# First projection of a two-layer hybrid diffusion backbone: order of loads, three blocks split, low weights by VectorE two blocks ahead

## The chip, the cores and the metric

One core of a Trainium2 chip runs the whole network in one launch. The metric is the device time in microseconds (us); smaller is better. The engines named are TensorE (PE), VectorE (DVE), ScalarE (ACT), GpSimd (POOL) and SyncE (SP), whose queue issues the loads.

## The reference

512 latent tokens (x) and 256 context tokens (ctx), width 1024, two layers, all in float32. Each layer is a mixer and a SwiGLU of 2816, each behind an RMS norm whose result is shifted and scaled by a modulation computed from a conditioning vector, one for x and another for the context. Layer 0's mixer is half gated linear attention in both directions, half grouped attention with rotary positions; layer 1's is windowed attention.

```python
mod_x = (sc @ ada_w[l] + ada_b[l])[:, None, :]        # sc = silu(c); mod_c from c_ctx
sh1x, sc1x, g1x, sh2x, sc2x, g2x = jnp.split(mod_x, 6, axis=-1)
hx = modulate(rms_norm(x, norm1_g[l]), sh1x, sc1x)    # h * (1 + scale) + shift
hc = modulate(rms_norm(xc, norm1_g[l]), sh1c, sc1c)
...
gq, gkk, gv, gg, lr_f, lr_b, bq, bk, bv = split_cols(h @ w_in, EVEN_WIDTHS)
dec_f = jax.nn.log_sigmoid((lr_f @ gk_w[0] + gk_b[0]).astype(jnp.float32)) / GLA_TAU
```

## The kernel before

The network is a stream of weight blocks of 128 output columns (`BLOCKS`), numbered n; layer 0's input projection is blocks 0 to 18 (`FIRST[("out", 0)]` is 19). Activations lie transposed, features on partitions, tokens along the free axis; a block multiplies eight 128x128 weight tiles with all 768 tokens and 2 columns that carry the shifts. Float32 accuracy comes from three products of rounded halves: each operand is split into a high part (a cast, `fp32r`) and a low part (operand minus high part). So a block is 8 x 3 products on 770 columns.

For each block: SP loads the raw weights into a ring of three (`load_raw`, L512); ScalarE casts the high part (`high`, L650); GpSimd subtracts the low part (L619), in place over the raw weights; TensorE multiplies (`block_products`, L1724) into one of two PSUM tiles `lin`; VectorE evacuates with the norm's factor (`scaled_out`, L1114 and L1115); ScalarE adds the shift's share (`mixer_projection`, L728). Block n+2 waits for block n's evacuation (`ev`).

The norm's factor is applied after the product, so that products can start before it is known. At the start the modulation is made in four groups (`ada_mm` L1669, two 1 MB loads each; `ada_copy` L657; `ada_T` L1679; `ada_reduce` L1050); the first two give the scale (`mod_scale`, `modA`, L1081). ScalarE casts the scaled x tiles (L702, L706), VectorE makes their low parts (L1126, L1131), and `first_blocks` (L1744) multiplies blocks 0 and 1, latent tokens (part 0) first, context tokens and shift columns (part 1) after the mean square (`mean_square`, L1777). Squares are L664, their sums L1091.

The rest of the modulation ("late tiles") is made on VectorE beside the projections: `late_modulation` (L1066), two products of 128x1024 for a tile in layer 0, with `c_activated` (L719) ahead on ScalarE. `LATE_AT` says how many of them stand in each block: before the evacuation from block 5 on, behind it up to block 4. Their loads (`load_late`, L525) use a ring of three, so tile i waits on SP until tile i-3 is done, and the raw load behind it in SP's order waits too.

Between blocks run the parts of the linear attention: `logits` (PE L1997; ACT L749, L750), `minus_exponential` (L754), `logarithm` (L758), `decays` and `references` on VectorE (L1368 to L1384), `relative` (L600) and `queries_scaled` (L608) on GpSimd, `bounded` (L1389), `exponentials` (L762, L763), transposes of values (L2003) and keys (L2009), `means` (L2015) and roots for the heads' norms (L785, L787), `given` (L1277) for the states handed to each chunk. Each engine runs its instructions strictly in the order in which they are written; the order around each block is written by hand with the block's number.

## Time and profile before

| | |
|---|---|
| median of 3 runs | 1618.42 us (1618.2 to 1618.67) |
| the profiled execution | 1620.3 us, span 1618.5 us |
| TensorE busy | 1557.9 us, 96% of the span |
| VectorE, ScalarE, GpSimd busy | 887.0, 544.6, 591.7 us |
| first block product | 23.49 us |
| first projection's blocks 2 to 18 | 49.7 to about 228 us |

A profile is one execution; the table's spans are of that one. Engines' timelines are read as: start, duration, engine and line, operation, what it writes and reads, how often, and in brackets how long the engine was idle before and what ended that. The kernel's later parts (attention, SwiGLU, layer 1) are not touched by the change, except where the given states are made.

### The profile page before, as it was taken

To read this page: it belongs to the slowest core of one execution; us is meant where nothing else is said; L and a number is where in the kernel's file an instruction comes from. 1 tells how busy PE (TensorE), PEld (TensorE's weight loads), DVE (VectorE), ACT (ScalarE), POOL (GpSimd) and SP (SyncE) were. 2 spreads that over 40 slices of the span, in tenths; PEclk is the share of its full clock that TensorE was granted. 3 is DMA by queue.
4 is the path that set the end of the run, shared out by engine and by line. 5 is a ranking of instruction groups with operands and counts; after the bars stand their busy time and mean duration, and the time that the engine had idled before them with its cause. 6 is when DMAs were issued, how large, how long until landed. Compare 5 with 4: busy or idle time off the path is not lost.

```text
span 1618.5 us, 25145 instructions
## 1 busy us (share of the span) xinstructions
PE 1557.9 (96%) x10716; PEld 1285.7 (79%) x10716; DVE 887.0 (55%) x1250; ACT 544.6 (34%) x711; POOL 591.7 (37%) x263
## 2 busy tenths in 40 slices
PE   6999999889999999999999999999999999999997
PEld 3887764467888888888888888865579998998995
DVE  5699776568577766665566433666643221221324
ACT  4743424453422211221122233245544322322232
POOL 1263235602333222322222222355644444444442
PEclk9999999999999999999999999999999999999998
DMA  8523110034233333333433222200022222223232
GB/s 340 197 104 118 41 40 1 1 133 143 71 116 127 131 130 115 119 131 130 144 120 127 92 75 69 66 27 1 1 66 86 95 95 91 92 92 104 92 97 99
DMA packets 41775, 158.54 MB, mean 98 GB/s; under 512 B 4768, under 2 KB 5152, under 8 KB 39872
## 3 DMA queue, kind: packets, MB, share of 16 engines
q1 hardware_dynamic: 41232, 156.74, 28.1%
q8 instruction: 85, 1.39, 0.4%
q0 software_dynamic: 432, 0.20, 0.1%
q14 instruction: 26, 0.21, 0.0%
HBM read 154.95 MB, written 2.10 MB: 97 GB/s over the span
## 4 chain that ended last, share of the span: by engine, by line
PE 72%; DVE 3%; issue 2%; ACT 1%; POOL 1%; DVEq 0%; POOLq 0%
PE psum L1724 65%; PE psum L1928 2%; PE psum L1896 1%; DVE osb L1305 1%; PE psum L1829 1%; POOL acc L593 1%; DVE product L1066 0%; PE psum L1944 0%; DVE mx L1200 0%; PE psum L1913 0%; PE psum L1902 0%; PE psum L1900 0%; PE psum L1898 0%; DVE xT L1547 0%; PE psum L1801 0%
## 5 line engine op out<-in xcount | busy, mean ns | idle before, releaser
L1724 PE MATMUL psum<-act,whi 128*128 128x258 f32 (+2 forms) x4000 | 792.1, 318 | 6.6 <-DVE xT L1547 4.5
L619 POOL TENSOR_TENSOR wlo<-raw,whi 128x1024 fp32r<-128x1024 f32 (+1 forms) x181 | 443.6, 2451 | 917.7 <-ACT whi L650 917.7
L1724 PEld LDWEIGHTS psum<-act,whi 128*128 128x128 f32 x4000 | 592.9, 189 | 66.7 <-issue 11.7
L1724 PE MATMUL psum<-act,wlo 128*128 128x512 f32 (+1 forms) x2000 | 476.3, 317 | 0.0
L1066 DVE SCALAR_TENSOR_TENSOR product<-adr,cb 128x1024 f32<-128x1024 f32 x128 | 281.8, 2234 | 134.9 <-DMA adr<-adat_dram 129.5
L1724 PEld LDWEIGHTS psum<-act,wlo 128*128 128x128 f32 x2000 | 311.5, 189 | 27.1
L650 ACT ACTIVATE whi<-raw 128x1024 fp32r<-128x1024 f32 (+1 forms) x181 | 188.1, 1039 | 330.2 <-DMA raw<-weights_dram 329.8
L1114 DVE SCALAR_TENSOR_TENSOR tmps<-psum,rs 128x256 f32<-128x256 f32 (+1 forms) x176 | 78.1, 485 | 199.7 <-PE psum L1724 195.2
L1724 PE MATMUL psum<-gh,whi 128*128 128x512 f32 (+1 forms) x528 | 160.9, 358 | 0.0
L1724 PE MATMUL psum<-gh,wlo 128*128 128x512 f32 (+1 forms) x528 | 160.8, 359 | 0.0
L1724 PE MATMUL psum<-gl,whi 128*128 128x512 f32 (+1 forms) x528 | 159.3, 355 | 0.0
L1547 DVE SCALAR_TENSOR_TENSOR xT<-psum,mod,xT 128x512 f32<-128x512 f32 x96 | 60.4, 656 | 160.2 <-PE psum L1724 155.7
L1200 DVE TENSOR_REDUCE mx<-psum 128x4 f32<-128x1024 f32 (+2 forms) x68 | 78.8, 1159 | 49.3 <-PE psum L1829 37.7
L1006 ACT ACTIVATE gh<-tmps 128x768 fp32r<-128x768 f32 (+1 forms) x44 | 32.5, 739 | 211.2 <-DVE tmps L1627 211.2
L593 POOL TENSOR_TENSOR acc<-acc,probT 128x1024 f32<-128x1024 f32 (+2 forms) x47 | 90.8, 1931 | 27.1 <-ACT probT L886 22.2
L1724 PEld LDWEIGHTS psum<-gh,whi 128*128 128x128 f32 x528 | 87.8, 188 | 15.9
L1724 PEld LDWEIGHTS psum<-gl,whi 128*128 128x128 f32 x528 | 87.1, 188 | 16.5
L1724 PEld LDWEIGHTS psum<-gh,wlo 128*128 128x128 f32 x528 | 86.7, 188 | 15.4
L1002 ACT ACTIVATE tmps<-tmps,bsm 128x512 f32<-128x512 f32 x66 | 40.7, 648 | 151.1 <-DVE bsm L1115 151.1
L886 ACT ACTIVATE probT<-psum 128x1024 f32<-128x1024 f32 (+2 forms) x80 | 66.9, 848 | 62.1 <-PE psum L1902 42.8
L1928 PE MATMUL psum<-probT,vtok 128*64 128x512 f32 (+2 forms) x320 | 72.6, 532 | 1.9 <-ACT probT L886 1.2
L728 ACT ACTIVATE big<-big,bsm 128x512 f32<-128x512 f32 (+1 forms) x50 | 29.3, 626 | 98.1 <-DVE bsm L1115 98.1
(185 smaller groups left out, 1212.2 us busy)
## 6 DMA issues: line engine op xcount, KB each, us to landing
raw<-weights_dram SPq DMA_DIRECT2D x181, 512.0 KB, 3.5
adr<-adat_dram SPq DMA_DIRECT2D x80, 512.0 KB, 4.5
ada_w<-ada_dram SPq DMA_DIRECT2D x8, 1024.0 KB, 15.1
xT<-x_in_dram SPq DMA_DIRECT2D x4, 1536.0 KB, 13.2
cb<-crow_dram SPq DMA_DIRECT2D x2, 1024.0 KB, 8.5
out_dram<-big SPq DMA_DIRECT2D x8, 256.0 KB, 2.1
con<-consts_dram SPq DMA_DIRECT2D x1, 512.0 KB, 7.4
con<-consts_dram SPq DMA_DIRECT2D x1, 320.0 KB, 3.5
```

The costliest lines, as they stand in the source:

```text
L593: nc.gpsimd.tensor_tensor(acc[L][:, :, qa:qb], so_far, probT[L][:, t % NPT, :, qa:qb], ALU.add) \
L619: nc.gpsimd.tensor_tensor(wlo[:, s, 0:w], raw[:, s, 0:w], whi[:, s, 0:w].bitcast(F32), ALU.subtract).then_inc(sem("s_lo"), 1)
L650: A(whi[:, s, 0:w], raw[:, s, 0:w], ACT.Copy).then_inc(sem("s_hi"), 1)
L886: A(probT[L][:, t % NPT, :, qa:qb], scored[t % 2][:, :, qa:qb], ACT.Exp, scale=SCALE) \
L1002: last = A(t, t, ACT.Silu, bias=bsm[:, n % 4, c:c + 1])
L1006: A(gh[L][:, b["i"], 0:b["tok"]], tmps[:, 6 + b["h"] % 2, 0:b["tok"]], ACT.Copy) \
L1066: STT(out=products[t % 2][:, :], in0=w, scalar=1.0, in1=cb[:, c, :], op0=ALU.mult, op1=ALU.mult, accum_out=mod[:, layer, d, c:c + 1]).then ...
L1114: STT(out=tiles[:, a:e], in0=ps, scalar=factor, in1=rs[:, a:e], op0=ALU.mult, op1=ALU.mult)
L1200: V.reduce_max(mx[:, i % 3, piece["slot"], rows_, :].rearrange("p q g -> p g q"), s_, AX.X) .then_inc(sem("a_mx"), 1)
L1547: ins = STT(out=xT[:, m, a:e], in0=lin[n % 2][:, a:e], scalar=mod[:, L, gate + m, c:c + 1], in1=xT[:, m, a:e], op0=ALU.mult, op1=ALU.add)
L1724: last = MM(out_[:, o:o + t1 - t0], w_, a_[:, t0:t1], start=k == order[0] and j == 0, stop=k == order[-1] and j == 2)
L1928: last = MM(bank(6)[r, qa:qb], vtok[L][:, kt, r], probT[L][:, t % NPT, g, qa:qb], start=a == 0, stop=a == len(u["steps"]) - 1, skip_group_ ...
```

## The change

- Loads: x and the context are loaded apart, x's 512 columns first and in two halves of the tiles, the first half in front of the second pair of modulation loads; raw weights 0 to 2 come earlier.
- Raw weights 3 go to a place of their own (`stage`), so they don't wait for the ring.
- The modulation groups use one half of one PSUM tile each (`wk[0]`), so group c waits for group c-1's copy and reduction; `wk[1]` holds block 2's first products.
- Scale and x tiles are made by halves: after the first group, tiles 0 to 3; after the second, 4 to 7. Blocks 0, 1 and 2 are all multiplied in parts by `first_blocks`, between the modulation groups.
- Low weights of blocks 0 to 18 are made on VectorE (`weights_low`), those of block n+2 behind the evacuation of block n and in front of block n's late tiles where n is below 5; GpSimd makes them from block 19 on.
- Logits, exponentials and logarithms of the decays come one block later; decays and references move behind the evacuation of blocks 5 and 6; the copies into `lrs` and `gks` likewise in block 2.
- `LATE_AT` spreads the 16 late tiles otherwise. `given` is made by halves, the last two halves still at the start of the attention.

```diff
@@ -42,7 +42,7 @@
 LATE = [(0, d) for d in [*range(16, 24), *range(32, 40), *range(24, 32), *range(40, 48)]] + [(1, d) for d in range(48)]
-LATE_AT = [0, 0, 3, 3, 1, 0, 0, 1, 1, 0, 2, 2, 2, 1, 0, 0, 0, 0, 0]
+LATE_AT = [0, 0, 2, 3, 2, 0, 0, 2, 2, 1, 1, 1, 1, 1, 0, 0, 0, 0, 0]
@@ -301,6 +301,7 @@
         gates = big[:, 8:12, :]
+        stage = at("stage", [P, KT * P], G + 14 * TILE)
@@ -421,9 +422,11 @@
+        first_out = [lin[0], lin[1], wk[1]]
...
-            ps = lin[n % 2]
+            ps = first_out[n] if n < 3 else lin[n % 2]
@@ -529,23 +532,28 @@
             x_tiles = x_in.rearrange("p (k t) -> p k t", k=KT)
-            for h in range(ADA_RING):
-                load_ada(h)
+            load_ada(0)
+            load_ada(1)
             load_raw(0)
-            sp.dma_start(xT[:, 0:half, :], x_tiles[:, 0:half, :]).then_inc(sem("s_xa"), 16)
-            sp.dma_start(xT[:, half:KT, :], x_tiles[:, half:KT, :]).then_inc(sem("s_xb"), 16)
+            sp.dma_start(xT[:, 0:half, 0:NX], x_tiles[:, 0:half, 0:NX]).then_inc(sem("s_xa"), 16)
             load_raw(1)
+            load_raw(2)
+            load_ada(2)
+            load_ada(3)
+            sp.dma_start(xT[:, half:KT, 0:NX], x_tiles[:, half:KT, 0:NX]).then_inc(sem("s_xb"), 16)
+            sp.dma_start(xT[:, :, NX:T], x_tiles[:, :, NX:T]).then_inc(sem("s_xc"), 16)
...
                 load_ada(h)
-            load_raw(2)
+            sp.dma_start(stage[:, :], weights[RING, :, :]).then_inc(sem("s_stage"), 16)
             sp.wait_ge(sem("s_adamm"), 2 * len(ADA_EARLY))
+            sp.dma_start(gkw[0:32, :], gkw_in).then_inc(sem("s_rope"), 16)
...
             sp.dma_start(con[:, 0:CC_ID], consts[:, 0:CC_ID]).then_inc(sem("s_rope"), 16)
-            sp.dma_start(gkw[0:32, :], gkw_in).then_inc(sem("s_rope"), 16)
             for n in range(RING, NB):
-                load_raw(n)
+                if n > RING:
+                    load_raw(n)
@@ -615,9 +623,10 @@
                 w = BLOCKS[n]["nk"] * P
-                pool.wait_ge(sem("s_hi"), n + 1)
-                nc.gpsimd.tensor_tensor(wlo[:, s, 0:w], raw[:, s, 0:w], whi[:, s, 0:w].bitcast(F32),
-                                        ALU.subtract).then_inc(sem("s_lo"), 1)
+                if n >= FIRST[("out", 0)]:
+                    pool.wait_ge(sem("s_hi"), n + 1)
+                    nc.gpsimd.tensor_tensor(wlo[:, s, 0:w], raw[:, s, 0:w], whi[:, s, 0:w].bitcast(F32),
+                                            ALU.subtract).then_inc(sem("s_lo"), 1)
@@ -644,17 +653,20 @@
                 w = BLOCKS[n]["nk"] * P
-                act.wait_ge(sem(f"s_raw{s}"), 16 * (n // RING + 1))
+                if n == RING:
+                    act.wait_ge(sem("s_stage"), 16)
+                else:
+                    act.wait_ge(sem(f"s_raw{s}"), 16 * (n // RING + (0 if s == 0 and n > RING else 1)))
...
                     act.wait_ge(sem("s_acc"), n - RING + 1)
-                A(whi[:, s, 0:w], raw[:, s, 0:w], ACT.Copy).then_inc(sem("s_hi"), 1)
+                A(whi[:, s, 0:w], stage[:, :] if n == RING else raw[:, s, 0:w], ACT.Copy).then_inc(sem("s_hi"), 1)
...
                     act.wait_ge(sem("s_adaT"), c - 1)
-                A(adasb[:, c % 2, :], wk[0][:, 512 * (c % 2):512 * (c % 2) + 512], ACT.Copy) \
+                A(adasb[:, c % 2, :], wk[0][:, 0:512], ACT.Copy) \
@@ -693,20 +705,23 @@
             ada_copy(0)
-            ada_copy(1)
             high(0)
-            act.wait_ge(sem("s_modA"), 1)
...
                 if k % 4 == 0:
+                    act.wait_ge(sem("s_modA"), 2 if k else 1)
...
                     .then_inc(sem("s_nhx"), 1)
-            high(1)
+                if k == 3:
+                    high(1)
+                    high(2)
+                    ada_copy(1)
+            act.wait_ge(sem("s_xc"), 16)
...
             for k in range(KT):
-                if k == 2:
+                if k == 4:
@@ -793,15 +808,14 @@
                     nc.scalar.preload_act_table_set(LN_EXP)
-                if n in (2, 3):
-                    logits(2 * n - 4)
-                    logits(2 * n - 3)
-                if n in (2, 3):
-                    minus_exponential(2 * n - 4)
-                    minus_exponential(2 * n - 3)
                 if n in (3, 4):
-                    logarithm(2 * n - 6)
-                    logarithm(2 * n - 5)
+                    logits(2 * n - 6)
+                    logits(2 * n - 5)
+                    minus_exponential(2 * n - 6)
+                    minus_exponential(2 * n - 5)
+                if n in (4, 5):
+                    logarithm(2 * n - 8)
+                    logarithm(2 * n - 7)
@@ -975,7 +989,10 @@
                     attention(1)
-                high(n + 2)
+                if n == 0:
+                    high(RING)
+                if n >= 3:
+                    high(n + 2)
@@ -991,6 +1008,8 @@
                         mixer_projection(L, n, b)
+                    if n == 1:
+                        high(n + 3)
@@ -1115,16 +1134,28 @@
             dve.wait_ge(sem("s_par"), 16)
-            for c in range(2):
-                ada_reduce(c)
-            dve.wait_ge(sem("s_mod"), 2)
-            mod_scale(0)
-            dve.wait_ge(sem("s_modA"), 1)
-            for k in range(KT):
-                hi, lo = [act_tile("proj", 0, k, low) for low in range(2)]
-                dve.wait_ge(sem("s_nhx"), k + 1)
-                STT(out=lo[:, 0:NX], in0=xT[:, k, 0:NX], scalar=modA[:, 0, k, 0:1], in1=hi[:, 0:NX].bitcast(F32),
-                    op0=ALU.mult, op1=ALU.subtract).then_inc(sem("s_nlx"), 1)
+            def weights_low(n):
+                s = n % RING
+                dve.wait_ge(sem("s_hi"), n + 1)
+                TT(wlo[:, s, :], stage[:, :] if n == RING else raw[:, s, :], whi[:, s, :].bitcast(F32), ALU.subtract) \
+                    .then_inc(sem("s_lo"), 1)
+            for h in range(2):
+                ada_reduce(h)
+                dve.wait_ge(sem("s_mod"), h + 1)
+                mod_scale(0, 4 * h, 4 * h + 4)
+                if h == 0:
+                    weights_low(0)
+                dve.wait_ge(sem("s_modA"), h + 1)
+                for k in range(4 * h, 4 * h + 4):
+                    hi, lo = [act_tile("proj", 0, k, low) for low in range(2)]
+                    dve.wait_ge(sem("s_nhx"), k + 1)
+                    STT(out=lo[:, 0:NX], in0=xT[:, k, 0:NX], scalar=modA[:, 0, k, 0:1], in1=hi[:, 0:NX].bitcast(F32),
+                        op0=ALU.mult, op1=ALU.subtract).then_inc(sem("s_nlx"), 1)
+                if h == 0:
+                    weights_low(1)
+                    weights_low(2)
@@ -1133,9 +1164,10 @@
                     dve.wait_ge(*nq("sq", 0, 1))
+                if k == 4:
+                    ada_reduce(2)
                 add_square(0, k, T)
-            for c in range(2, 4):
-                ada_reduce(c)
+            ada_reduce(3)
@@ -1268,14 +1300,13 @@
-            def given(d):
-                dve.wait_ge(sem("g_carry"), 2 * d + 2)
-                if d == 1:
-                    dve.wait_ge(sem("g_sr"), 1)
-                ref_ = gpos[:, 0, 2 * d:2 * d + 2, 1:NCH].unsqueeze(3).to_broadcast([P, 2, NCH - 1, CH])
-                TT(statr[d][:, 1:NCH, :, :].rearrange("p c g v -> p g c v"),
-                   states[d][:, :, :, 0:NCH - 1].rearrange("p g v c -> p g c v"), ref_, ALU.mult) \
+            def given(d, g):
+                dve.wait_ge(sem("g_carry"), 2 * d + g + 1)
+                if d == 1 and g == 0:
+                    dve.wait_ge(sem("g_sr"), 2)
+                ref_ = gpos[:, 0, 2 * d + g, 1:NCH].unsqueeze(2).to_broadcast([P, NCH - 1, CH])
+                TT(statr[d][:, 1:NCH, g, :], states[d][:, g, :, 0:NCH - 1].rearrange("p v c -> p c v"), ref_, ALU.mult) \
@@ -1402,13 +1434,6 @@
-                if n == 2:
-                    low_rank_low()
-                if n in (5, 6):
-                    for i in (2 * n - 10, 2 * n - 9):
-                        decays(i)
-                    for i in (2 * n - 10, 2 * n - 9):
-                        references(i)
@@ -1564,6 +1591,8 @@
                     dve.wait_ge(*nq("rs", q, 1))
+                if n == 1:
+                    weights_low(RING)
@@ -1594,9 +1623,18 @@
                     scaled_out(n, proj_tile(L, m), DK ** -0.5 if L == 0 and m in (3, 4) else 1.0)
+                    if n == 2:
+                        low_rank_low()
+                    if 2 <= n < FIRST[("out", 0)] - 2:
+                        weights_low(n + 2)
...
                             late_modulation(i)
+                    if n in (5, 6):
+                        for i in (2 * n - 10, 2 * n - 9):
+                            decays(i)
+                        for i in (2 * n - 10, 2 * n - 9):
+                            references(i)
@@ -1660,23 +1698,23 @@
-                if c >= 2:
-                    pe.wait_ge(sem("s_adacp"), c - 1)
+                if c >= 1:
+                    pe.wait_ge(sem("s_adacp"), c)
...
                     for g in range(4):
-                        last = MM(wk[0][32 * g:32 * g + 32, 512 * (c % 2):512 * (c % 2) + 512],
+                        last = MM(wk[0][32 * g:32 * g + 32, 0:512],
...
                 pe.wait_ge(sem("s_adacp"), c + 1)
-                if c >= 2:
-                    pe.wait_ge(sem("s_mod"), c - 1)
+                if c >= 1:
+                    pe.wait_ge(sem("s_mod"), c)
                 for q in range(4):
-                    last = TR(wk[1][:, 512 * (c % 2) + P * q:512 * (c % 2) + P * q + P],
+                    last = TR(wk[0][:, 512 + P * q:512 + P * q + P],
@@ -1725,16 +1763,16 @@
-            def first_blocks(n, part):
-                out_ = lin[n % 2]
+            def first_blocks(n, part, tiles=range(KT)):
+                out_ = first_out[n]
...
                     pe.wait_ge(sem("s_shift"), 2)
-                for k in range(KT):
+                for k in tiles:
@@ -1780,18 +1820,25 @@
             ada_mm(0)
+            ada_T(0)
+            first_blocks(0, 0, range(0, 4))
             ada_mm(1)
-            ada_T(0)
+            first_blocks(1, 0, range(0, 2))
             ada_T(1)
-            first_blocks(0, 0)
+            first_blocks(1, 0, range(2, 4))
+            first_blocks(2, 0, range(0, 4))
+            first_blocks(0, 0, range(4, 8))
             ada_mm(2)
-            first_blocks(1, 0)
+            first_blocks(1, 0, range(4, 6))
+            ada_T(2)
+            first_blocks(1, 0, range(6, 8))
             ada_mm(3)
-            ada_T(2)
+            first_blocks(2, 0, range(4, 6))
             ada_T(3)
+            first_blocks(2, 0, range(6, 8))
             mean_square(0, T)
-            first_blocks(0, 1)
-            first_blocks(1, 1)
+            for n in range(3):
+                first_blocks(n, 1)
@@ -2018,9 +2065,11 @@
-                if n in (2, 3):
-                    logits(2 * n - 4)
-                    logits(2 * n - 3)
+                if n in (3, 4):
+                    logits(2 * n - 6)
+                    if n == 3:
+                        pe.wait_ge(*ev(2))
+                    logits(2 * n - 5)
```

## Rows read from the trace of the kernel before

**Rows 1.** The page: busy time by engine, and the chain that ended last by line.
```profile
PE 1557.9 (96%) x10716; PEld 1285.7 (79%) x10716; DVE 887.0 (55%) x1250; ACT 544.6 (34%) x711; POOL 591.7 (37%) x263
...
PE psum L1724 65%; PE psum L1928 2%; PE psum L1896 1%; DVE osb L1305 1%; PE psum L1829 1%; POOL acc L593 1%; DVE product L1066 0%; PE psum L1944 0%; DVE mx L1200 0%; PE psum L1913 0%; PE psum L1902 0%; PE psum L1900 0%; PE psum L1898 0%; DVE xT L1547 0%; PE psum L1801 0%
```

**Rows 2.** A stretch of the start: busy time by engine, granted clock, DMA share, GB/s.
```profile
23.40:28.00 4.60, 4.51 (x11) 3.57 (x12) 4.59 (x7) 4.53 (x8) 0.01 (x1) 0.50 1.02 422
```

**Rows 3.** TensorE's timeline, from the modulation to block 3.
```profile
10.72 1.93 PE L1669 MATMUL psum<-ada_w,cpad 128*32 128x512 f32 x8 [0.71 <-DMA ada_w<-ada_dram]
...
23.49 1.19 PE L1744 MATMUL psum<-act,whi 128*128 128x512 f32 x2 [4.45 <-DVE act L1126]
...
31.43 1.92 PE L1669 MATMUL psum<-ada_w,cpad 128*32 128x512 f32 x16
...
42.18 1.46 PE L1777 MATMUL psum<-big,con 128*128 128x512 f32 x4
43.45 0.51 PE L1744 MATMUL psum<-act,whi 128*128 128x258 f32 x2
...
49.74 0.95 PE L1724 MATMUL psum<-act,whi 128*128 128x512 f32 x4 [0.25 <-issue]
...
59.02 0.86 PE L1724 MATMUL psum<-act,whi 128*128 128x512 f32 x4
```

**Rows 4.** TensorE's timeline: its six waits from block 5 to block 13.
```profile
77.71 0.94 PE L1724 MATMUL psum<-act,whi 128*128 128x512 f32 x4 [0.88 <-issue]
...
87.02 0.95 PE L1724 MATMUL psum<-act,whi 128*128 128x512 f32 x4 [0.60 <-ACT whi L650]
...
104.62 0.94 PE L1724 MATMUL psum<-act,whi 128*128 128x512 f32 x4 [0.41 <-DVE bsm L1115]
...
142.46 0.87 PE L2009 MATMUL psum<-con,gsc 128*128 128x128 f32 x6 [1.89 <-ACT hrs L787]
...
152.27 0.87 PE L2009 MATMUL psum<-con,gsc 128*128 128x128 f32 x6 [1.07 <-DVE vtok L1181]
...
165.97 0.88 PE L2009 MATMUL psum<-con,gsc 128*128 128x128 f32 x6 [2.40 <-ACT kgt L773]
```

**Rows 5.** VectorE's timeline: late tiles, decays, evacuation of block 7.
```profile
59.51 1.21 DVE L1066 SCALAR_TENSOR_TENSOR product<-adr,cb 128x1024 f32<-128x1024 f32 x1
...
61.79 3.42 DVE L1066 SCALAR_TENSOR_TENSOR product<-adr,cb 128x1024 f32<-128x1024 f32 x1
...
93.01 0.94 DVE L1368 SCALAR_TENSOR_TENSOR dec<-dec,gsc 128x768 f32<-128x768 f32 x1
94.05 1.76 DVE L1376 TENSOR_TENSOR_SCAN gsc<-cmask,dec 128x768 f32<-128x768 f32 x1
...
107.62 1.02 DVE L1114 SCALAR_TENSOR_TENSOR big<-psum,rs 128x512 f32<-128x512 f32 x2
```

**Rows 6.** ScalarE's timeline: x tiles, c's activation, logits, the cast of weights 5.
```profile
21.76 5.20 ACT L702 ACTIVATE act<-xT,modA 128x512 fp32r<-128x512 f32 x8 [2.48 <-DVE modA L1081]
...
56.77 1.92 ACT L719 ACTIVATE cb<-cb 128x2048 f32<-128x2048 f32 x1
...
61.98 0.89 ACT L749 ACTIVATE gsc<-psum,par 128x768 f32<-128x768 f32 x1
...
73.90 1.07 ACT L650 ACTIVATE whi<-raw 128x1024 fp32r<-128x1024 f32 x1 [7.20 <-DMA raw<-weights_dram]
```

**Rows 7.** GpSimd's timeline: the subtraction of weights 5, two decay differences.
```profile
75.04 2.57 POOL L619 TENSOR_TENSOR wlo<-raw,whi 128x1024 fp32r<-128x1024 f32 x1 [10.92 <-ACT whi L650]
...
97.96 5.07 POOL L600 TENSOR_TENSOR dec<-gsc,gd 128x768 f32<-128x768 f32 x2
```

**Rows 8.** SP's timeline (late tiles, raw weights 5), and the page's raw loads.
```profile
61.91 7.11 SPq L525 DMA_DIRECT2D adr<-adat_dram  x3
69.06 0.43 SPq L512 DMA_DIRECT2D raw<-weights_dram  x1
...
raw<-weights_dram SPq DMA_DIRECT2D x181, 512.0 KB, 3.5
```

27 lines of the change are left out of this document (16 added, 11 removed).

## The prediction

> **What bounds the kernel now.** I read the page's busy line and its chain that ended last first [rows 1]: TensorE is busy 96% of the span, and its block products (L1724) alone are 65% of the chain. So a change in the first projection is worth what it takes from, or adds to, TensorE's idle time and its start, and nothing else. Then I read the timelines of the first 170 us, engine by engine.
>
> The start: TensorE has modulation matmuls while the first weights of the modulation stream in (10.72), then waits 4.45 us for VectorE's first low tile and begins the first block at 23.49; from there it is busy almost without a break to block 2 at 49.74 and block 3 at 59.02 [rows 3]. Its clock is at the lower level, 0.50, in 23.4 to 28 us [rows 2]. After block 3 it waits six times, 7.3 us in all: 0.88, 0.60, 0.41, 1.89, 1.07 and 2.40 us [rows 4]. The last three wait for ScalarE or VectorE copies that come late because VectorE evacuated the blocks late. That VectorE is late is to be seen in its timeline: from 59.5 us on it runs almost without a pause; block 8 waits 0.41 us for the evacuation of block 6, whose products were over 9 us before, and block 7 is evacuated at 107.62 [rows 4, 5]. So VectorE is nearly co-critical from block 3 to block 13; that is where this change decides.
>
> **The start, worked out.** The DMA engines move 422 GB/s in this stretch [rows 2], about 2.5 us for 1 MB. In the new order the first half of x's latent columns lands at about 14.5 us, raw weights 1 and 2 by 17, the third and fourth modulation loads by 22. The first modulation group (ends 12.7 [rows 3]), its copy, transposes and reduction take about 2.3 us, so modA's first half is there at 15.0. ScalarE then casts x tiles at 0.65 us each (5.20 for 8) [rows 6]. VectorE puts the first low weights in front (1.15 us, below), so its first low x tile ends at 16.9 and TensorE starts block 0 at 17.1, 6.4 us before the 23.49 of now. What moves behind that start: the second modulation group (16 matmul records, 1.92 us at the full clock) and its transposes (0.7 us). What is new is block 2's latent part there. TensorE from 17.1: twelve matmuls at the lower clock at 0.43 us (5.1; 11 in 4.6 us [rows 2]), then sixty at 0.23 (14.0; block 2's 24 products of 770 columns take 8.5 us, 512 of them 0.23 each), three modulation groups (5.8), three sets of transposes (2.2), the mean square (1.3, 42.18 to 43.45), three context parts of 2.9 us each (49.34 less 43.45 is two of them; 8.8) [rows 3], and about 0.6 us of waiting for the third copy, which stands behind four squares on ScalarE. End: 17.1 + 37.8 = 54.9. Block 3 began at 59.02 with 0.72 us of logits in front of it, which now come later; without them 58.3. The front gains 3.4 us. Its bounds: if the copies behind the squares are later, 2 us less; if the clock rises sooner, 1.5 us more.
>
> **The vector queue, worked out.** Removed: nineteen subtractions on GpSimd (2.4 us each), which were off the path but held VectorE: a 1024-wide two-input operation takes 1.21 us alone and 3.42 us beside one of them [rows 5]. Added: the same subtraction on VectorE, an operation this engine does not show at this width. Bounds: 1.15 us apart by the two-input rows of the same width, 2.4 us as on GpSimd; I take 1.15, the same engine and width. Per block VectorE pays 1.15 and is spared up to 2.2. GpSimd's four decay differences (5.07 for two) and four query products stay [rows 7], and by the same comparison I charge about 1.2 us for each where VectorE has two-input work; with none of it, 9.4 us less.
>
> But each subtraction waits on VectorE for ScalarE's cast, and behind it stand the late modulation tiles (2.3 us each, two products of 1.15). Those tiles release the next loads on SP's queue, which lie in front of the next raw load: a ring through SP, DMA, ScalarE and VectorE. Now SP shows it: three tile loads stretched over 7.11 us, the raw load only at 69.06, landed at 73.90, 4.8 us later (median of the kernel 3.5) [rows 8]; ScalarE waits 7.20 us for it [rows 6], but VectorE does not. Followed through:
> - Block 2 ends at 54.7. c's activation on ScalarE stands behind the load of block 4's weights (issued at 51.8) and ends at 59.6 (58.7 now) [rows 6]. Tiles 0 and 1: to 64.2. Block 3 (ends 63.4) evacuated at 65.2.
> - Raw weights 5 are issued at 64.7, land at 69.5, are cast at 70.6. VectorE stands 5.4 us. Subtraction to 71.8, tiles 2 to 4 to 78.7, block 4 evacuated at 79.7.
> - Raw weights 6 are issued once tile 3 is done (76.4) and land at 81.6; cast 82.7. VectorE stands 3.0 us. Subtraction 83.9 (block 6 can start: 87.02 now), tiles 5, 6 to 88.5, block 5 at 89.5.
> - The cast of weights 7 stands behind an evacuation, four logits operations (0.78 apart), two exponentials and two logarithms: 91.2. VectorE stands 1.7 us; subtraction 92.4.
> - Decays of two (2 x 2.7) and references (0.5): 98.3 [rows 5]. Block 6 evacuated 99.3, subtraction with GpSimd beside it 101.7, decays 108.7, clamps 110.9, tiles 7, 8 with GpSimd 116.6, block 7 evacuated 117.6. Now that ends at 108.6 [rows 5].
>
> TensorE needs block 7 evacuated for block 9, and its own low weights 1.2 us later. Its idle time: 1.9 us in front of block 5 (the third and fourth logits need ScalarE's copies of the first two, which stand behind the cast at 70.6), 0.3 at block 6, 1.0 at block 8 (102.0), then, its block 8 ending at 110.6, 8.2 us at block 9 (118.8; 113.1 now). Behind it 1.8, 1.0 and 0.3 us for the value transposes and the mean, whose inputs come from blocks 8 and 9 evacuated late. By block 11 only one late tile stands in each block instead of two, VectorE has caught up, and the 1.89, 1.07 and 2.40 us of now are gone: the first key transposes of block 13 come at about 169.5 against 165.97. In all -3.4 (front) + 14.5 (new idle) - 7.3 (idle of now) = +3.8 us.
>
> A stall of 8 us has a second price. Behind the 4.45 us wait that ended at 23.49 the granted clock is 0.50, the lower of its two levels (1.2 and 2.4 GHz), for some 5 us of matmuls [rows 2, 3]. Behind 8.2 us I expect the lower level again: about 2.4 us lost in block 9, of which 1.8 lie under the wait for the value transposes: +0.5. The trace agrees with a rule of the Trainium skill, page "TensorE: Matmul & The Clock Gate", section "Part 1: The HAM clock gate": the throttled clock is the default, and activity releases it. The rule speaks against this change.
>
> **Edits costed at nothing.** The given states by halves: the same elements, two instructions for one (0.1 us more each), in blocks 17 and 18 where VectorE pauses and TensorE does not wait. The ring's "place" for weights 3 moves no work. gkw before c's rows: 64 KB. The late tiles' new order keeps their number, 16.
>
> **Total.** The profiled run took 1620.3 us with a span of 1618.5; the median is 1618.42, the span's own size, so I add the difference to the median: 1618.4 + 3.8 + 0.5 = 1622.7, said as 1622.5.
>
> **The rivals.**
> - The vector queue keeps up (B). If raw weights land in the median 3.5 us, GpSimd's eight operations cost VectorE nothing and the new waits shrink, block 7 is evacuated at about 111 and block 9 starts near 112 to 114. Following the same chain, the first key transposes of block 13 come about 4.6 us before 165.97: 1613.8. For it: GpSimd's subtractions cost VectorE up to 2.2 us each now, and all go. Against it: the 4.8 us landing and the stretched 7.11 us were seen behind the same loads. With no new wait at all it would be 1618.4 - 3.4 - 7.3 = 1607.7; nothing shows how SP could be that early.
> - The two cancel (C): block 9 starts at about 115 to 116, the front's 3.4 us are given back and no more: 1618.
> - Slower for good (D): the stall not only at block 9 but the backlog lasting beyond block 13. It decides if a subtraction takes nearer to 2.4 than to 1.15 us: 1.25 more in some eight blocks is 10 us of vector work, of which about half comes through: 1627.5.
> - The change does not do what it says: TensorE's first block does not start earlier, since the loads of x land later than worked out, with block 0 at 20 instead of 17.1. Then 2.9 us more of A, inside the range.
>
> **How the numbers follow.** A (forecast, 1622.5, own range 1619 to 1626) 0.50; B 0.22; C 0.20; D 0.08. A measurement of this kernel can tell about 0.2% from no change, 3.2 us: faster is below 1615.2, slower above 1621.7. Of A, 0.13 lies below that line. Faster 0.22, same 0.20 + 0.13 = 0.33, slower 0.37 + 0.08 = 0.45. The range reaches down to B's value and a little beyond, up to nearly D's: 1613.5 to 1627. What is left out is the deep end of B and the high side of D.
>
> **What would show it.** In the changed profile: TensorE's first block product at 17.1 (right within 1 us) and block 3 at 54.9; VectorE idle in front of its subtractions, released by ScalarE's cast, 5 us near 65 and 3 us near 80; raw weights 5 cast at about 70; a TensorE wait for VectorE near 110 of about 8 us, with a lower granted clock behind it; the waits of 1.89, 1.07 and 2.40 us gone. If the wait near 110 is under 3 us the forecast is wrong, and then I expect VectorE's own operations at their uncontended lengths, and block 9 before 114. If block 3 comes later than 56.5, the front was over-priced.

## The result and the profile of the changed kernel

| | before | changed |
|---|---|---|
| time, median (range), us | 1618.51 (1618.2 to 1619.24) | 1624.71 (1622.38 to 1626.09) |
| ratio, 95% interval | | 1.0035 [1.0023, 1.0046] |
| profiled execution: time, span, us | 1620.3, 1618.5 | 1622.38, 1620.3 |

The changed kernel is slower by 0.35%, about 5.7 us (the medians differ by 6.2). The forecast was 1622.5 (own range 1619 to 1626). The profiled execution is the lowest of the changed kernel's five, so the two traces show less of a difference (1.8 us of span) than the medians.

The page: busy time, the costliest group of TensorE (idle time in front of it, and what ended it), and the median landing of a raw load (last column, us).

```profile
PE 1558.8 (96%) x10716; PEld 1288.2 (80%) x10716; DVE 890.9 (55%) x1272; ACT 544.6 (34%) x711; POOL 539.9 (33%) x244
...
L1762 PE MATMUL psum<-act,whi 128*128 128x258 f32 (+2 forms) x3968 | 788.2, 319 | 11.7 <-DVE wlo L1141 7.3
...
raw<-weights_dram SPq DMA_DIRECT2D x180, 512.0 KB, 3.5
```

Against [rows 1]: TensorE is busy as before, GpSimd 51.8 us and nineteen instructions less, VectorE only 3.9 us more, although it has taken these nineteen subtractions over. The idle time in front of the block products now stands for the most part in one place, 7.3 us.

TensorE's timeline at the start answers to [rows 3]; the two stretches behind it (granted clock third from the end, GB/s last) answer to [rows 2].

```profile
13.27 1.12 PE L1717 MATMUL psum<-con,adasb 128*128 128x128 f32 x4 [0.71 <-ACT adasb L669]
17.02 1.19 PE L1782 MATMUL psum<-act,whi 128*128 128x512 f32 x2 [2.64 <-DVE act L1154]
...
44.63 0.59 PE L1782 MATMUL psum<-act,whi 128*128 128x258 f32 x2
...
53.48 0.75 PE L1762 MATMUL psum<-act,whi 128*128 128x512 f32 x3
```

```profile
17.00:19.70 2.70, 2.68 (x6) 2.15 (x7) 2.70 (x4) 2.57 (x4) 0.00 (x0) 1.00 1.02 425
19.70:23.00 3.30, 3.30 (x23) 1.41 (x21) 1.43 (x2) 0.00 (x0) 0.00 (x0) 1.00 1.00 392
```

The granted clock reads 1.00 in both stretches, and yet the six matmuls of the first lie 0.43 us apart, as under 0.50 in [rows 2]; soon behind 19.7 us they lie 0.23 apart. Here the durations are to be read, not the column.

Block 0 starts at 17.02 instead of 23.49 and block 3 at 53.48 instead of 58.3 (59.02 less 0.72 us of logits, which now stand later). The front gains 4.8 us in this pair of traces. In the seven traces with this start (the changed kernel, e1, e2, e3, e4, e7, e10) block 3 begins at 52.76 to 53.48; in the four with the start of the kernel before (itself, e5, e6, e9) the work in front of it, logits left out, ends at 57.59 to 58.76.

All TensorE waits over 0.3 us from block 3 to block 13; they answer to [rows 4]:

```profile
72.29 0.62 PE L2044 MATMUL psum<-lrs,gks 96*128 96x512 f32 x2 [0.98 <-ACT dec L765]
...
73.87 0.62 PE L2044 MATMUL psum<-lrs,gks 96*128 96x512 f32 x2 [0.97 <-ACT dec L765]
...
117.18 1.62 PE L1762 MATMUL psum<-act,whi 128*128 128x512 f32 x4 [7.26 <-DVE wlo L1141]
...
139.95 0.74 PE L2050 MATMUL psum<-con,big 128*128 128x128 f32 x5 [1.43 <-DVE vgt L1429]
```

Four waits, 10.6 us, where there were six with 7.3 us. The one that matters is block 9's, which waits for its low weights on VectorE. What VectorE did before that answers to [rows 5]:

```profile
69.68 1.23 DVE L1141 TENSOR_TENSOR wlo<-raw,whi 128x1024 fp32r<-128x1024 f32 x1 [5.02 <-ACT whi L662]
...
81.86 1.23 DVE L1141 TENSOR_TENSOR wlo<-raw,whi 128x1024 fp32r<-128x1024 f32 x1 [3.08 <-ACT whi L662]
...
90.09 1.23 DVE L1141 TENSOR_TENSOR wlo<-raw,whi 128x1024 fp32r<-128x1024 f32 x1 [1.42 <-ACT whi L662]
...
98.15 1.55 DVE L1141 TENSOR_TENSOR wlo<-raw,whi 128x1024 fp32r<-128x1024 f32 x1
99.62 2.22 DVE L1400 SCALAR_TENSOR_TENSOR dec<-dec,gsc 128x768 f32<-128x768 f32 x1
...
108.89 2.48 DVE L1085 SCALAR_TENSOR_TENSOR product<-adr,cb 128x1024 f32<-128x1024 f32 x1
...
114.87 1.01 DVE L1133 SCALAR_TENSOR_TENSOR big<-psum,rs 128x512 f32<-128x512 f32 x2
...
115.87 1.21 DVE L1141 TENSOR_TENSOR wlo<-raw,whi 128x1024 fp32r<-128x1024 f32 x1
```

VectorE stands three times, 9.5 us, in front of a subtraction and for ScalarE's cast. From 90.09 on it works without a gap: decays, references, clamps, the late tiles 7 and 8 (107.75 to 114.87), the evacuation of block 7, then block 9's low weights, ready at 117.0. So block 9's start is 90.1 plus 27 us of queue. The casts themselves wait for raw weights, and these for SP (they answer to [rows 6] and [rows 8]):

```profile
68.59 1.06 ACT L662 ACTIVATE whi<-raw 128x1024 fp32r<-128x1024 f32 x1 [7.27 <-DMA raw<-weights_dram]
...
80.77 1.06 ACT L662 ACTIVATE whi<-raw 128x1024 fp32r<-128x1024 f32 x1 [5.49 <-DMA raw<-weights_dram]
```

```profile
51.16 12.85 SPq L528 DMA_DIRECT2D adr<-adat_dram  x3
64.06 0.43 SPq L515 DMA_DIRECT2D raw<-weights_dram  x1
```

SP issues three tile loads, each when VectorE has freed a buffer, over 12.85 us, and only then the raw weights 5, at 64.06; their cast starts at 68.59.

The granted clock of the changed kernel (third figure from the end), behind the two short waits and behind the long one:

```profile
74.00:76.00 2.00, 2.00 (x9) 1.72 (x10) 2.00 (x5) 1.28 (x2) 0.00 (x0) 0.67 0.72 252
76.00:78.00 2.00, 2.00 (x8) 1.71 (x8) 2.00 (x5) 0.00 (x0) 0.00 (x0) 0.50 0.73 209
...
110.00:114.00 4.00, 0.00 (x0) 0.00 (x0) 4.00 (x5) 0.00 (x0) 2.71 (x2) 0.78 0.37 113
114.00:118.00 4.00, 0.82 (x3) 0.76 (x4) 4.00 (x9) 2.02 (x4) 0.09 (x1) 0.50 0.85 301
118.00:124.00 6.00, 6.00 (x24) 5.16 (x24) 6.00 (x6) 2.98 (x4) 5.63 (x2) 0.63 0.34 125
```

What a stretch loses is the time that TensorE was busy times (1 less the clock): 0.7 and 1.0 us from 74 to 78, 0.4 us from 117.2 to 118, 2.2 us from 118 to 124, in all 4.3 us. The kernel before has a clock of 1.00 in every stretch from 28.4 to 239 us.

A mark behind all of this is the same pair of attention matmuls in both kernels, first in the kernel before, then in the changed one:

```profile
239.10 0.44 PE L1852 MATMUL psum<-identr,mxr 128*128 128x128 f32 x2 [1.45 <-DVE mxr L1212]
```

```profile
242.41 0.44 PE L1899 MATMUL psum<-identr,mxr 128*128 128x128 f32 x2 [1.45 <-DVE mxr L1244]
```

From block 3 to that mark, the kernel before (its two logits in front of block 3 left out), then the changed one:

```profile
59.02:239.10 180.08, 170.43 (x1317) 139.92 (x1315) 154.94 (x209) 73.45 (x102) 72.25 (x30) 1.00 0.26 88
```

```profile
53.48:242.41 188.93, 174.97 (x1321) 143.91 (x1319) 155.66 (x228) 78.01 (x106) 30.68 (x15) 0.96 0.25 87
```

The changed kernel is 3.3 us later there. The sum: -4.8 (front) + 10.6 (waits now) - 7.3 (waits before) + 0.9 (small waits, 1.8 against 0.9) + 4.3 (clock) = +3.7 us, 0.4 us more than measured. "The mark" means this place below.

### The profile page after: what moved, and what is told of

Its sections match the earlier page's. It is cut to its first block, busy times and chain, and to the rows that moved or that the text cites. A ratio compares the mean times of both kernels' runs of the same rounds, so it can differ in the third digit from the quotient of the medians.

```text
span 1620.3 us, 25160 instructions
## 1 busy us (share of the span) xinstructions
PE 1558.8 (96%) x10716; PEld 1288.2 (80%) x10716; DVE 890.9 (55%) x1272; ACT 544.6 (34%) x711; POOL 539.9 (33%) x244
## 4 chain that ended last, share of the span: by engine, by line
PE 71%; DVE 3%; issue 2%; ACT 1%; POOL 0%; DVEq 0%; POOLq 0%
PE psum L1762 65%; PE psum L1975 2%; PE psum L1943 1%; DVE osb L1336 1%; PE psum L1876 1%; POOL acc L601 0%; DVE product L1085 0%; PE psum L1991 0%; DVE mx L1232 0%; PE psum L1960 0%; PE psum L1949 0%; PE psum L1947 0%; PE psum L1945 0%; DVE xT L1574 0%; PE psum L1848 0%
## 5 line engine op out<-in xcount | busy, mean ns | idle before, releaser
L628 POOL TENSOR_TENSOR wlo<-raw,whi 128x1024 fp32r<-128x1024 f32 (+1 forms) x162 | 389.6, 2405 | 797.0 <-ACT whi L662 797.0
L1085 DVE SCALAR_TENSOR_TENSOR product<-adr,cb 128x1024 f32<-128x1024 f32 x128 | 278.5, 2208 | 132.2 <-DMA adr<-adat_dram 125.5
```

Of the source, the lines that this page charges most:

```text
L628: nc.gpsimd.tensor_tensor(wlo[:, s, 0:w], raw[:, s, 0:w], whi[:, s, 0:w].bitcast(F32), ALU.subtract).then_inc(sem("s_lo"), 1)
L1085: STT(out=products[t % 2][:, :], in0=w, scalar=1.0, in1=cb[:, c, :], op0=ALU.mult, op1=ALU.mult, accum_out=mod[:, layer, d, c:c + 1]).then ...
```

## The experiments

The theory: the front's gain is given back at block 9, because VectorE's queue up to the evacuation of block 7 is too long. Two things are supposed to make it so: VectorE stands for casts (the ring through SP, DMA, ScalarE and VectorE), and two late tiles stand in block 7 beside GpSimd's differences. The rivals: W, the subtractions are simply too much work for VectorE; that the tiles' places don't matter; H, the order of the loads brings nothing. Each ratio is to the kernel before on the same chip, with the 95% interval.

### e1_raw_first: raw weights ahead of the tiles on SP's queue

```diff
                 if n <= len(LATE_AT):
-                    for i in late_tiles(n - 1):
+                    for i in late_tiles(n - 2):
```

> The changed kernel with one edit on SP's queue: the late tiles of block n-2 instead of n-1 are issued behind the raw load of block n, so a raw load no longer stands behind tile loads that wait for VectorE's products. Theory A (a ring through SP, DMA, ScalarE and VectorE makes VectorE stand 9.5 us): its waits for the casts of weights 5 and 6 (5.0 and 3.1 us) go, the evacuation of block 7 comes about 8 us earlier (107 instead of 114.9), the wait of TensorE at block 9 falls from 7.3 to 2 to 4 us, time 1613 to 1618. Rival W (it is the added vector work, 1.15 us a block, not the waiting): the waits go, but the work behind them fills up, block 9 waits over 6 us, time 1622 or more. Rival F (the split front is itself no gain): no change to speak of in the start, and the time stays above 1618.5 even with the wait at block 9 gone.

1616.91 us (1615.22 to 1619.35), ratio 0.998 [0.9971, 0.9988]; the mark at 233.93. VectorE's subtraction for block 7's weights and TensorE's block 9:

```profile
81.57 1.22 DVE L1141 TENSOR_TENSOR wlo<-raw,whi 128x1024 fp32r<-128x1024 f32 x1
```

```profile
108.66 0.94 PE L1762 MATMUL psum<-act,whi 128*128 128x512 f32 x4 [2.90 <-DVE wlo L1141]
```

From 50 to 120 us none of VectorE's subtractions waits for a cast any more; this one runs at 81.57 and not at 90.09. Block 9's wait falls from 7.26 to 2.90 us. So the ring is a cause, and VectorE does nineteen subtractions in a kernel that is faster than before: W does not hold.

### e4_late_later: no late tile in blocks 7 and 8

```diff
-LATE_AT = [0, 0, 2, 3, 2, 0, 0, 2, 2, 1, 1, 1, 1, 1, 0, 0, 0, 0, 0]
+LATE_AT = [0, 0, 2, 3, 2, 0, 0, 0, 0, 1, 2, 2, 2, 2, 0, 0, 0, 0, 0]
```

> The changed kernel with four late tiles moved out of blocks 7 and 8 into blocks 10 to 13 (0, 0, 2, 3, 2, 0, 0, 0, 0, 1, 2, 2, 2, 2). Theory A: the waits for casts stay (5.0, 3.1, 1.4 us), the evacuation of block 7 comes 4.6 to 7 us earlier (two tiles and what GpSimd adds to them), block 9 waits 0 to 3 us instead of 7.3, TensorE's clock stays at its upper level there, and waits like the 1.89, 1.07 and 2.40 us of before come back at blocks 11 to 13; time 1616 to 1621. Rival W: the same sum of vector work only shifts the wait to blocks 11 to 13, time 1623 or more.

1616.78 us (1614.79 to 1620.08), ratio 0.9981 [0.9972, 0.9989]; the mark at 233.58. The edit takes the two tiles out of block 7 and the two out of block 8, and puts one more into each of blocks 10 to 13. VectorE's cast waits stay as they were (4.88, 2.89 and 1.42 us). TensorE's second logits wait and block 9, and the clock between:

```profile
73.45 0.62 PE L2044 MATMUL psum<-lrs,gks 96*128 96x512 f32 x2 [0.97 <-ACT dec L765]
...
109.74 0.94 PE L1762 MATMUL psum<-act,whi 128*128 128x512 f32 x4 [1.52 <-DVE wlo L1141]
```

```profile
74.00:76.00 2.00, 2.00 (x13) 1.74 (x12) 2.00 (x3) 0.87 (x2) 0.00 (x0) 1.00 0.67 244
```

With the two tiles out of block 7, block 9's wait is 1.52 us although the cast waits remain. So the second cause is shown too, and either cure alone turns the result into a gain of 0.2%. Of the difference between these two traces, 1.7 us are not the edit's: up to block 7 both kernels have the same instructions, and the clock behind the logits waits fell in the one and stayed at 1.00 in the other.

### e10_after_old_tiles: the tile distribution of the kernel before

```diff
-LATE_AT = [0, 0, 2, 3, 2, 0, 0, 2, 2, 1, 1, 1, 1, 1, 0, 0, 0, 0, 0]
+LATE_AT = [0, 0, 3, 3, 1, 0, 0, 1, 1, 0, 2, 2, 2, 1, 0, 0, 0, 0, 0]
```

The entries are blocks 0, 1, 2 and so on. Against the changed kernel one tile more stands in block 2 (three), one less in blocks 4, 7, 8 and 9, and one more in blocks 10 to 12. The text below leaves out blocks 2 and 9 to 12, and its "third tile", which it puts into block 3, is block 2's.

> The changed kernel with the distribution of late tiles of the kernel before (three in block 3, one in block 4, one each in blocks 7 and 8 instead of two). If the stall in front of block 9 is made by the tiles that stand in VectorE's queue ahead of the evacuation of block 7 (theory), one tile and 2.3 to 3.6 us beside GpSimd go from blocks 5 to 8: the wait in front of block 9 shrinks from 7.3 to 3 to 5 us and the total is 1619 to 1622; the wait in front of block 4's or 5's low weights may grow by 1 us, for the third tile stands in block 3 again. If the tiles' places don't matter and the added subtractions do (rival), the wait stays over 7 us and the total at 1624.

1619.07 us (1618.43 to 1621.82), ratio 1.0 [0.9991, 1.0009]; the mark at 237.64.

```profile
90.17 1.22 DVE L1141 TENSOR_TENSOR wlo<-raw,whi 128x1024 fp32r<-128x1024 f32 x1 [1.11 <-ACT whi L662]
...
111.40 1.01 DVE L1133 SCALAR_TENSOR_TENSOR big<-psum,rs 128x512 f32<-128x512 f32 x2
```

```profile
74.83 1.01 PE L2044 MATMUL psum<-lrs,gks 96*128 96x512 f32 x2 [3.82 <-ACT dec L765]
...
113.99 0.94 PE L1762 MATMUL psum<-act,whi 128*128 128x512 f32 x4 [0.70 <-issue]
```

This is the cleanest pair. VectorE's queue starts at the same time (90.17 against 90.09) and has one tile less: block 7 is evacuated 3.47 us earlier (111.40 against 114.87) and block 9 starts 3.2 us earlier. The expected total of 1619 to 1622 was met at its lower edge, block 9's wait (3 to 5 us) was not: it is 0.70, because TensorE itself arrives later. The rival, that the tiles' places don't matter, wanted over 7 us there and does not hold. The third tile in block 2 holds the raw weights on SP longer, ScalarE casts them at 71.14 instead of 68.59, and the logits copies behind this cast cost TensorE 3.82 us. The granted clock behind that wait is 0.70 in 74 to 76 us, 0.50 in 76 to 78 and 0.55 in 78 to 82, worth another 2.9 us. So the change without its new tile distribution is no slower than before; what the front brought is then lost in front of block 5.

### e5_before_spread and e9_before_late_later: the two distributions in the kernel before

```diff
-LATE_AT = [0, 0, 3, 3, 1, 0, 0, 1, 1, 0, 2, 2, 2, 1, 0, 0, 0, 0, 0]
+LATE_AT = [0, 0, 2, 3, 2, 0, 0, 2, 2, 1, 1, 1, 1, 1, 0, 0, 0, 0, 0]   # e5
+LATE_AT = [0, 0, 2, 3, 2, 0, 0, 0, 0, 1, 2, 2, 2, 2, 0, 0, 0, 0, 0]   # e9
```

> The kernel before with the changed kernel's distribution of the late tiles alone (0, 0, 2, 3, 2, 0, 0, 2, 2, 1, 1, 1, 1, 1), all else as before. Theory A (the two tiles in blocks 7 and 8 stand in front of evacuations that TensorE needs): the evacuation of block 7 comes at 110 to 112 instead of 108.6, that of block 8 at 122 to 124 where block 10 wants it at 123.4, the waits of 1.07 and 2.40 us at blocks 12 and 13 shrink since one tile stands there instead of two, in all -1 to +3 us, 1617.5 to 1621.5 on the scale of 1618.5. Rival B2 (the distribution is the gain, and only the subtraction on VectorE spoils it): -3 us or more.

> The kernel before with the later distribution of the late modulation tiles (none in blocks 6 to 8, two each in blocks 10 to 13), nothing else changed. If two tiles in blocks 7 and 8 hurt the changed kernel only because its two decays and its subtractions meet there (theory), the kernel before gains little: its block 7 is evacuated up to 4 us earlier, which takes its wait of 0.41 us in front of block 8 and part of the 1.89, 1.07 and 2.40 us behind, 0 to -4 us, and the two tiles of blocks 12 and 13 give some of it back. If the later distribution is simply better wherever it stands (rival), the gain is the same here as in the changed kernel, -8 us: 1610 to 1612.

e5: 1625.3 us (1624.82 to 1625.68), ratio 1.003 [1.0018, 1.0041]. e9: 1622.23 us (1620.38 to 1623.42), ratio 1.0012 [1.0003, 1.0021]. TensorE in e5, then in e9:

```profile
105.57 1.62 PE L1724 MATMUL psum<-act,whi 128*128 128x512 f32 x4 [2.66 <-DVE bsm L1115]
...
140.60 1.75 PE L2003 MATMUL psum<-con,big 128*128 128x128 f32 x7 [6.10 <-ACT vgt L769]
```

```profile
106.73 0.95 PE L1724 MATMUL psum<-act,whi 128*128 128x512 f32 x4 [2.67 <-DVE bsm L1115]
```

Both expectations missed, on the same side. The distribution of the change costs the kernel before 0.3%, as much as the whole change, where -1 to +3 us was expected, and the rival B2, by which it is a gain, does not hold. The two tiles of block 7 push the evacuation behind them from 107.62 to 114.32, and the copies for the value transposes come 6.10 us late; this wait is not in e9, which has no tile there. The waits of 2.66 and 2.67 us in front of block 8 (0.41 in [rows 4]), and one of 1.12 us in front of block 7, are in both kernels, so they go with what the two distributions share, the tiles of blocks 2 to 4. e9, which helps the changed kernel by 8 us, costs the kernel before about 2 us (ratio 1.0012). So neither distribution is good or bad in itself. Moving tiles moves SP's loads with them; what counts in these traces is which evacuation or cast stands behind them.

### e2_low_last: the subtraction behind the late tiles

```diff
-                    if 2 <= n < FIRST[("out", 0)] - 2:
-                        weights_low(n + 2)
                     if n < 5:
                         for i in late_tiles(n):
                             late_modulation(i)
+                    if 2 <= n < FIRST[("out", 0)] - 2:
+                        weights_low(n + 2)
```

> The changed kernel with one edit on VectorE's queue: in blocks 2 to 4 the subtraction of the low weights stands behind the late tiles, not in front of them; SP's order is as in the changed kernel. Theory A: VectorE does tiles instead of standing; what it wanted of raw weights 5 comes as late as before or a little earlier, VectorE's waits for casts fall from 9.5 to under 2 us in all, the evacuation of block 7 comes 7 to 8 us earlier, block 9 waits 2 to 4 us, time 1614 to 1618. Rival W: as the changed kernel, 1622 or more, since the work is the same. Rival S (the fault is SP's order alone, whatever VectorE does): no gain here, since the raw load still stands behind the tile loads.

1621.14 us (1619.51 to 1624.33), ratio 1.0006 [0.9998, 1.0015]; the mark at 237.58.

```profile
64.59 1.43 PE L1762 MATMUL psum<-act,whi 128*128 128x512 f32 x4 [2.15 <-issue]
...
112.32 1.38 PE L1762 MATMUL psum<-act,whi 128*128 128x512 f32 x4 [2.88 <-DVE wlo L1141]
```

The time is a miss (1614 to 1618 was expected). VectorE's waits for casts are gone and block 9's wait shrank to 2.88 us, both as expected, and with SP's order unchanged the kernel is 0.3% faster than the changed one; so rival S does not hold. But the evacuation of block 7 came 4.9 us sooner and not 7 to 8 (110.01), and block 4's low weights now stand behind two tiles (they run at 63.27, and TensorE waits 2.15 us for them); that was not seen. In this order part of the one wait is traded for the other; e1 has the same wait at block 9 (2.90 us) without the one at block 4, whose weights VectorE subtracts at 56.34 there.

### e3_pool_low: the subtractions back on GpSimd

```diff
-                if n >= FIRST[("out", 0)]:
+                if n >= 4:
                     pool.wait_ge(sem("s_hi"), n + 1)
+                    pool.wait_ge(sem("s_lo"), n)
...
-                    if 2 <= n < FIRST[("out", 0)] - 2:
-                        weights_low(n + 2)
```

> The changed kernel with GpSimd subtracting the low weights from block 4 on, as in the kernel before; the front, SP's order and all else as changed. Theory A: VectorE has nothing that waits for a cast, and pays up to 2.2 us beside each subtraction as before; the 7.3 us wait at block 9 shrinks to 0 to 3, the front's 3.3 us are kept, 1614 to 1617. Rival W: the same or better, since all the added work goes; it can't be told from A by the time alone, but by VectorE's busy time up to block 9: W wants it lower than in the changed kernel, A expects it about the same or higher, as contention replaces the subtractions. Rival F: 1618.5 or more.

1625.24 us (1623.38 to 1629.88), ratio 1.0037 [1.0025, 1.0049]; the mark at 243.20. GpSimd's subtraction, VectorE's product beside it, and block 9:

```profile
69.71 2.91 POOL L629 TENSOR_TENSOR wlo<-raw,whi 128x1024 fp32r<-128x1024 f32 x1 [11.56 <-ACT whi L663]
```

```profile
70.31 3.39 DVE L1086 SCALAR_TENSOR_TENSOR product<-adr,cb 128x1024 f32<-128x1024 f32 x1
```

```profile
114.50 1.62 PE L1761 MATMUL psum<-act,whi 128*128 128x512 f32 x4 [4.58 <-DVE bsm L1135]
```

A miss, and the second run against W. From block 4 on VectorE has no subtraction and no cast wait, and yet the kernel is as slow as the changed one: block 9 still waits 4.58 us, and the value transposes another 3.80. A subtraction on GpSimd stretches the VectorE product beside it from 1.22 to 3.39 us, by 2.2 us, against the 1.15 us that VectorE pays for doing it itself. What VectorE no longer stands, it works: from 58 to 110 us it is busy 48.2 us, in the changed kernel 41.1. So handing the subtractions to VectorE is no loss. The expected 1614 to 1617 was missed because the evacuation of block 7 comes only 1.6 us sooner (113.27 against 114.87), although 9.5 us of waits are gone.

### e6_before_raw_first: e1's edit in the kernel before

```diff
                 if n <= len(LATE_AT):
-                    for i in late_tiles(n - 1):
+                    for i in late_tiles(n - 2):
```

> The kernel before with the edit of e1 on SP's queue (late tiles one block later in SP's order, so raw loads don't stand behind them). Theory A: in the kernel before nothing on VectorE waits for a cast, so only TensorE's waits of 0.88 and 0.60 us at blocks 5 and 6 can go, and ScalarE's 7.2 us wait for raw weights 5; -1.5 to 0 us. Rival G (raw-first is a gain by itself, whatever the order on VectorE, which would make e1's gain of about 9 us against the changed kernel no proof of the ring): -4 us or more.

1619.99 us (1619.03 to 1622.07), ratio 0.9999 [0.999, 1.0008]. TensorE's waits of 0.88 and 0.60 us [rows 4] are gone, and one grew by 0.7 us (0.41 before):

```profile
103.79 0.94 PE L1724 MATMUL psum<-act,whi 128*128 128x512 f32 x4 [1.15 <-DVE bsm L1115]
```

The raw weights were late in the kernel before too, but nothing on VectorE waited for them, so bringing them forward is worth nothing to speak of; rival G, a gain of 4 us or more, does not hold. The wait became one that costs only when the change put a waiting subtraction into VectorE's queue.

### e8_x_later: x behind all four first modulation loads

```diff
-            load_ada(0)
-            load_ada(1)
+            for h in range(ADA_RING):
+                load_ada(h)
             load_raw(0)
...
-            load_ada(2)
-            load_ada(3)
```

> The changed kernel with x's first half loaded behind all four first modulation loads, as before, instead of between them; x and context stay apart and the blocks split. Theory A (the front's gain of 4.8 us up to block 3 rests on x being there at 14.5 us): x's first half lands at about 19.3, block 0 starts at about 21 instead of 17.0, block 3 at 57 to 57.5 instead of 53.5, and since all behind hangs on it the time is 3 to 4.5 us over the changed kernel's, ratio to before 1.0055 to 1.0065. Rival H (the load order is hidden: TensorE makes it up while it waits at block 9 anyway): block 3 comes later but block 9 does not, ratio 1.0035.

1630.74 us (1627.77 to 1631.76), ratio 1.006 [1.0047, 1.0072].

```profile
21.54 1.19 PE L1780 MATMUL psum<-act,whi 128*128 128x512 f32 x2 [7.11 <-DVE act L1152]
...
121.91 1.41 PE L1760 MATMUL psum<-act,whi 128*128 128x512 f32 x3 [8.33 <-DVE wlo L1139]
```

Block 0 starts 4.5 us later, block 9 4.7 us later and the mark 4.7 us later (247.14). The front's gain is real and comes through to the end one for one; H does not hold.

### e7_both: e1 and e4 together

> The changed kernel with both edits of e1 (raw loads ahead of the late tiles) and e4 (no late tiles in blocks 7 and 8, two in 10 to 13). Theory A: both cut the same stall at block 9, so they don't add up in full: no wait at block 9, casts waited for under 1 us in all, about 1 us of waits at blocks 11 to 13; first product of the attention about 9 us before the kernel before, ratio 0.993 to 0.996 (1607.5 to 1612 on the scale of 1618.5). Rival W: the vector work is what it is, the ratio stays at 0.998 like each alone.

1609.91 us (1608.15 to 1611.89), ratio 0.9938 [0.9924, 0.9952]; the mark at 225.91. The group of block products on the page:

```profile
L1762 PE MATMUL psum<-act,whi 128*128 128x258 f32 (+2 forms) x3968 | 784.8, 318 | 4.5 <-DVE xT L1574 4.5
```

From the first block at 16.89 to 219 us TensorE has no wait over 0.3 us. The 4.5 us left in front of the block products stand for something else, far behind. The mark is 13.2 us before that of the kernel before: 4.8 us of front, 7.3 us of old waits, and small parts. This version beats both kernels, by 0.6% and by about 1%. The expectation took the two edits to cut the same stall and not to add up in full; in fact they nearly do (0.55% and 0.54% alone, 0.97% together). Rival W wanted 0.998 here and does not hold; nor does rival F, the front being no gain.

## Why the prediction was right, and where its steps were off

The time, the sign and the mechanism (A) came as forecast: the start earlier, the gain given back in one wait for VectorE in front of block 9. That the sum fits as well as it does (+4.3 against +3.7 us) is in part luck: the new waits were charged at 14.5 us and took 10.6, the clock was charged at 0.5 us and took 4.3, and these two errors cancel. Step by step:

- **Block 0 at 17.1, block 3 at 54.9.** Measured 17.02 and 53.48. The start was right to 0.1 us. The front gained 4.8 us and not 3.4. Block 3 came 36.5 us behind block 0, where 37.8 were charged. The lower clock lasted 2.7 us and not 5.1, the bound "the clock rises sooner", but the 72 products took 19.2 us all the same (19.1 charged): the first twelve 4.35, the other sixty 14.8 and not 14.0. Over-priced were the three sets of transposes (1.1 us, 2.2 charged), the wait for the third copy (0.6 charged, none over 0.2) and the mean square (1.1, 1.3 charged); the modulation groups took 6.2 and not 5.8. In e1, which starts alike, the slow matmuls lasted 4.0 us and block 3 began at 53.32, no later.
- **VectorE's waits of 5.4, 3.0 and 1.7 us.** Measured 5.02, 3.08 and 1.42. Raw weights 5 issued at 64.7 and cast done at 70.6: measured 64.06 and 69.65. The 4.8 us that I took for a raw load behind tile loads, and not the median of 3.5, was near: 4.5 us from issue to cast.
- **A subtraction takes 1.15 us.** Measured 1.13 to 1.14 apart where GpSimd is idle, 1.47 beside its difference. The end of 2.4 us, on which rival D rested, is excluded, and e3 shows D's price on the other engine.
- **1.9 us of idle time in front of block 5.** Measured 0.98 and 0.97 us. Their second price was not foreseen: the clock behind them, 1.7 us in this trace.
- **Block 7 evacuated at 117.6, block 9 at 118.8 behind a wait of 8.2 us.** Measured 115.9, 117.18 and 7.26. The 1.7 us came from the clamps (2.2 assumed, 0.94 measured), from a queue that began 1.2 us sooner (91.2 for 92.4, the third subtraction's end) and from the subtraction behind block 6's evacuation (2.4 assumed, 1.47 measured); the two tiles of block 7 were under-priced (5.7 assumed, 7.1 measured: 1.22, 2.48, 2.48 and 1.22).
- **0.3 us at block 6, 1.0 us at block 8.** Neither is there: block 6's weights were ready at 83.0 (83.9 worked out) and the evacuation of block 6 began 1.1 us sooner than worked out, and the lower clock in block 5 made TensorE later.
- **Behind block 9: 1.8, 1.0 and 0.3 us.** One wait is left, 1.43 us. The waits of 1.89, 1.07 and 2.40 us are gone, as forecast.
- **The clock behind the long wait, +0.5 us** (2.4 less 1.8 hidden). The 2.4 was near (2.6 measured). Together with the wait for the value transposes the forecast had 2.3 us, 1.8 and 0.5; measured were 1.43 and 2.6, so together they were 1.7 us under-priced; how much of the lost clock lay under the wait no run shows.
- **Rival B** (1613.8) needed the casts on time. e1 gives it: 0.998, about 1615 on the scale of 1618.5 (1616.91 on its own chip).
- **The total.** +4.3 us forecast for the profiled execution, +3.3 at the mark and +1.8 at the span's end. The medians differ by 6.2 us. About 2 us of that lie between executions of the changed kernel (spans of 1620.3 to 1624.0). Where, the trace of one execution can't say, so this stays open. Of the 3.3 us at the mark, 1.7 are made up in layer 0's attention: the out projection starts 1.9 us later (379.72 against 377.79) where the work at 320.22 had been 3.6 us later (323.83). About 1.1 us of that is the clock from 320 to 340 us (0.91 against 0.83). The steps above account for the 3.3 us at the mark, not for the 6.2.

What the prediction did not price is the tile distribution by itself. It charged the two tiles of block 7 inside the chain, but it listed the new order of the tiles among the edits costed at nothing, "keeps their number, 16". e10 shows that this line alone decides between 1.0000 and 1.0035, and e5 that it costs the kernel before 0.3%. The number of tiles is kept; their place ahead of an evacuation is not.

The Trainium skill, page "GPSIMD Engine Reference", section "Key points", had VectorE and GpSimd share SBUF interfaces for two-input work. The rows of e3 agree (1.22 against 3.39 us), and an evacuation, which reads PSUM, took 1.01 us there too beside a GpSimd difference (from 94.73, the difference from 94.70).

## What to carry to other kernels

When a step moves to an engine's in-order queue with a wait in front, follow the ring: what the wait needs, who issues that load, and which work behind the wait frees the loader; putting the awaited load ahead on the loader's queue was worth 0.55% here and nothing where nobody waited. A list that only says in which block side work is done is not free to rearrange: price each item by the evacuation or load that stands behind it. And test the parts of a losing change apart, since a real gain at the front (4.8 us) was hidden by two cheap faults behind it.
